# Both ends of the expert stage: first-round tables, token-order router logits, and the last pair's rows through a transposed one-hot matrix

## The chip, the cores and the metric

One core of a Trainium2 chip runs the whole program. Its engines are TensorE (PE in the profile, its weight loads PEld), VectorE (DVE), ScalarE (ACT), GpSimd (POOL) and SyncE (SP), with 16 DMA engines between SBUF and DRAM. Each engine works off its own instructions in order, and semaphores order the engines among each other. The metric is the device time of one execution in microseconds; lower is better.

## The reference, cut to what matters

Two layers over 384 tokens (128 of a prompt, 256 of a sample) of width 1024. Each layer has a mixer (layer 0: state space heads and long convolutions, layer 1: attention) and then a mixture of experts, and a final norm follows. The change is in the experts:

```python
g_prob = softmax(t @ w_gr + b_gr)                    # 4 groups
g_w, g_idx = top_k(g_prob, 1)
e_logits = (t @ w_er + b_er).reshape(n_tok, 4, 8)    # 8 experts in each group
e_prob = softmax(e_logits[g_idx])
e_w, e_idx = top_k(e_prob, 2)
weights = g_w * e_w / sum(e_w)                       # combine: (tokens, 32 experts)
hid = silu(t @ w_gate[e]) * (t @ w_up[e])            # hidden width 256
out = sum over e of (hid * combine) @ w_down[e]
x = x + gate * out                                   # gate: one row for prompt, one for sample
```

All arithmetic is fp32.

## The kernel before

Tokens lie in three tiles `t` of 128. The residual is `xR`, its normed and modulated transpose is `hT` (width on partitions).

**Head of the expert stage.** `router(l, t)` multiplies the 36 router columns `wr` (as TensorE's weights) with `hT`, so that the logits come out transposed. ACT copies them (`take_logits` on ACT) to `lgT`, and `logits(l, t)` turns them back on TensorE. DVE adds the bias (L2413) and picks for each token two experts, `ohs`, by a chain of small operations. From their sum `rmask` (`chosen`) TensorE counts each token's place within its expert, in `pos`, four fp32 matmuls against a triangle and ones. DVE makes a one-hot row of 384 slots for each token and choice (`onehots`, L2479, six operations). 72 bf16 matmuls of these with `rtok` give the table `tbl`: for each of 32 experts and six rounds of `CAP` = 64 slots the token that sits there. DVE decodes it into `tbli` (which row to gather, L2492, semaphore `table`) and `scati` (which row of the output to store to, `stores`). Meanwhile ACT writes the token rows `htok` to DRAM (`rows_out`).

**The stage.** Experts go in 16 pairs `n`, 64 slots for each of the two. Should an expert have more than 64 tokens, further rounds follow; here all pairs fit into one round (r = 8, 16 pairs). GpSimd gathers the rows of a pair to `xs` (indirect DMA). TensorE turns them (`turn`), multiplies with gate and up (`gate_up`), turns the hidden rows (`turn_hidden`) and multiplies with down (`down`). ACT and DVE share the copies from PSUM; the result of a pair is in `ob`, and GpSimd stores its rows to `outs_d` in DRAM (`scatter`, `store`; `expert_rows` in the trace). Weights come as blocks of 2 MB (three parts for each pair) on SP's queue, in `expert_loads`: `next_load` refills a place of the ring as soon as the matmuls that read it are done (`g_done`, `gu_done`, `down_done`). A third place for each part (`ahead`) and a fourth for gate (`late`) serve the first eight pairs only. In the order of SP's queue the last blocks are gate 14, up 14, down 13, gate 15, up 15, down 14, down 15.

**End of the stage.** TensorE does gate_up(15), down(14), turn_hidden(15), down(15), then spreads the residual gates (`gff`: a product of a row of ones with a gate row on one partition). GpSimd stores pairs 14 and 15. SP waits for both (`stored`) and loads all rows back by token, two for each token (`row_loads`, to `yg`). ACT weighs the first (`weigh`, L1921), DVE adds the weighed second (L2531), multiplies with the gate (L2534) and adds to `xR` (L2540), in six halves (`combine`). ACT measures the sum of squares (`measure`, `squares`), DVE makes the root (`root`), and the next layer's norm or the final norm follows. Loads of the next layer's projection wait for the last row load.

PSUM's eight banks are given out by a written plan (`bank_plan`): each job has a name, the engine that takes its result, and sometimes a bank; `open_bank` waits until the holder before is taken, `full` waits for TensorE, `took` for the taker. `link` waits for an operation of the same engine. In layer 0 the stage lies at about 585 to 850 us of the profile, in layer 1 at about 1097 to 1364 us.

## Time and profile before

| | us |
|---|---|
| median of three runs (1363.38 to 1369.64) | 1367.5 |
| profiled execution, its time | 1369.48 |
| profiled execution, its span | 1367.7 |
| PE busy | 1204.8 |
| DVE busy | 450.7 |
| ACT busy | 334.2 |
| POOL busy | 200.8 |

The time of a run is measured around the program; the span is from the first to the last instruction of the profiled execution. A busy matmul engine is not at its peak: the granted clock, 1.00 for 2.4 GHz and 0.50 for 1.2 GHz, says at what speed it ran (0.955 in the mean). An engine's busy time says little on its own; what ended an engine's wait, in the stretch in question, says what a change there is worth. A wait is shown as "idle before <- who ended it".

### The profile page before, as it was taken

Reading aid. Unit: us, or ns where it says so; the run is one execution under the profiler, and the core shown is the slowest. Engines: PE = TensorE matmul, PEld = TensorE weight load, DVE = VectorE, ACT = ScalarE, POOL = GpSimd, SP = SyncE. Lnnn points to the kernel's source line nnn. Section 1 sums busy time; section 2 is a strip of 40 time slices with the busy share of each in tenths; the row PEclk is TensorE's granted clock in tenths of the full one; section 3 lists DMA queues with packets and bytes.
Section 4 is the critical chain, followed back from the end, with each engine's and each line's share of the span. In section 5 each row is a group of like instructions: output and inputs, shape, how many; then the busy total and the mean of one; then the engine's idle time right before and its main releaser. Section 6 shows DMA issues by size and latency. Waiting matters only on the chain.

```text
span 1367.7 us, 16634 instructions
## 1 busy us (share of the span) xinstructions
PE 1204.8 (88%) x6374; PEld 677.0 (50%) x6374; DVE 450.7 (33%) x969; ACT 334.2 (24%) x850; POOL 200.8 (15%) x261
## 2 busy tenths in 40 slices
PE   4999998999999999959999775999789959989772
PEld 2456654554545554446545433753455546545430
DVE  1452078542338740431111105112573331111115
ACT  4212364210123200321111105123453321111113
POOL 1000022200125410011212102061001011212100
PEclk9999999999999999979999996999999979999996
DMA  9995510667910136369999986760315469999983
GB/s 340 347 387 192 184 31 1 229 236 252 349 62 1 62 148 247 121 233 420 417 416 419 420 367 248 284 65 0 139 63 179 172 231 420 419 416 419 419 355 146
DMA packets 94402, 336.91 MB, mean 246 GB/s; under 512 B 12784, under 2 KB 16598, under 8 KB 69633
## 3 DMA queue, kind: packets, MB, share of 16 engines
q1 hardware_dynamic: 73488, 303.18, 56.8%
q0 software_dynamic: 13952, 25.86, 6.9%
q10 hardware_dynamic: 6897, 6.97, 1.5%
q8 instruction: 45, 0.74, 0.2%
q14 instruction: 20, 0.16, 0.0%
HBM read 333.76 MB, written 23.18 MB: 261 GB/s over the span
## 4 chain that ended last, share of the span: by engine, by line
PE 70%; DMA 17%; DVE 6%; ACT 2%; POOL 2%; issue 2%; SPq 0%; ACTq 0%; DVEq 0%; POOLq 0%
PE bank L870 62%; DMA ring<-in_moe_w_down_dram 10%; PE bank L874 5%; DMA ring<-in_moe_w_up_dram 4%; PE bank L901 3%; DMA ring<-in_w_ada_dram 1%; DMA arena<-expert_rows 1%; PE bank L947 1%; POOL ring L2691 1%; POOL hT L2694 1%; DVE arena L2531 1%; DVE arena L2534 1%; ACT ring L2000 1%; DMA hT<-rows,scr 0%; POOL arena L2694 0%
## 5 line engine op out<-in xcount | busy, mean ns | idle before, releaser
L870 PE MATMUL bank<-ring,arena 128*64 128x256 f32 (+3 forms) x2624 | 439.4, 440 | 45.1 <-DMA ring<-in_moe_w_up_dram 18.2
L870 PEld LDWEIGHTS bank<-ring,arena 128*64 128x64 f32 (+1 forms) x2624 | 218.7, 146 | 229.6 <-issue 116.7
L870 PE MATMUL bank<-hT,ring 128*128 128x384 f32 (+4 forms) x960 | 301.2, 472 | 2.4 <-DVE hT L2129 1.7
L870 PEld LDWEIGHTS bank<-hT,ring 128*128 128x128 f32 (+1 forms) x960 | 177.7, 192 | 122.4 <-issue 18.0
L870 PE MATMUL bank<-arena 128*64 128x256 f32 (+7 forms) x800 | 117.3, 383 | 10.5 <-DVE arena L2479 4.5
L2506 DVE TENSOR_TENSOR hT<-hT,bank 128x256 f32<-128x256 f32 x32 | 13.5, 421 | 266.8 <-ACT hT L1887 266.8
L870 PEld LDWEIGHTS bank<-arena 128*64 128x64 f32 (+4 forms) x800 | 59.9, 150 | 52.0 <-issue 28.8
L1887 ACT ACTIVATE hT<-bank 128x256 f32<-128x256 f32 x32 | 12.3, 384 | 249.5 <-PE bank L870 249.5
L874 PEld LDWEIGHTS bank<-cst,hT 128*128 128x128 f32 x368 | 47.4, 190 | 48.0 <-issue 35.9
L874 PE MATMUL bank<-cst,hT 128*128 128x128 f32 x368 | 61.1, 301 | 11.3 <-DMA hT<-rows,scr 11.3
L870 PE MATMUL bank<-ring,hT 128*128 128x512 f32 x144 | 63.3, 599 | 0.4 <-ACT hT L2014 0.4
L2511 DVE COPY arena<-bank 128x512 f32<-128x512 f32 x32 | 22.1, 692 | 111.7 <-PE bank L870 111.7
L874 PE MATMUL bank<-cst,arena 128*128 128x128 f32 (+2 forms) x208 | 30.8, 293 | 29.3 <-DVE arena L2534 12.8
L870 PE MATMUL bank<-arena,ring 128*128 128x128 f32 (+2 forms) x272 | 46.8, 324 | 4.6 <-ACT arena L1963 1.8
L874 PEld LDWEIGHTS bank<-cst,arena 128*128 128x128 f32 (+2 forms) x208 | 25.9, 153 | 42.5 <-DVE arena L2534 14.7
L1898 ACT ACTIVATE arena<-bank 128x512 f32<-128x512 f32 x32 | 19.1, 597 | 113.6 <-PE bank L870 113.6
L870 PE MATMUL bank<-arena,cst 128*128 128x512 f32 (+5 forms) x76 | 35.3, 616 | 12.4 <-DVE arena L2452 9.4
L2749 POOL COPY scr<-arena 128x1 int32 x28 | 5.1, 182 | 271.5 <-ACT arena L1898 167.2
L870 PEld LDWEIGHTS bank<-ring,hT 128*128 128x128 f32 x144 | 27.5, 193 | 34.3 <-issue 33.3
L2733 POOL DMA_INDIRECT hT<-rows,scr x32 | 33.1, 1036 | 71.2 <-PE bank L874 27.2
L870 PEld LDWEIGHTS bank<-arena,ring 128*128 128x128 f32 (+2 forms) x272 | 32.1, 185 | 22.8 <-issue 9.2
L2739 POOL DMA_INDIRECT expert_rows<-arena,scr x32 | 32.6, 1019 | 60.1 <-POOL scr L2749 23.5
(315 smaller groups left out, 1131.9 us busy)
## 6 DMA issues: line engine op xcount, KB each, us to landing
ring<-in_moe_w_up_dram SPq DMA_DIRECT2D x28, 2048.0 KB, 20.8
ring<-in_moe_w_down_dram SPq DMA_DIRECT2D x28, 2048.0 KB, 19.5
ring<-in_w_ada_dram SPq DMA_DIRECT2D x24, 2048.0 KB, 16.0
ring<-in_moe_w_gate_dram SPq DMA_DIRECT2D x24, 2048.0 KB, 20.6
ring<-in_ev_w_in_dram SPq DMA_DIRECT2D x10, 2048.0 KB, 12.8
arena<-in_moe_w_gate_dram SPq DMA_DIRECT2D x8, 2048.0 KB, 14.6
ring<-in_ev_w_out_dram SPq DMA_DIRECT2D x4, 2048.0 KB, 17.3
arena<-in_moe_w_up_dram SPq DMA_DIRECT2D x4, 2048.0 KB, 20.3
```

What stands on the lines that cost most here:

```text
L870: return nc.tensor.matmul(out, lhsT, rhs, start=start, stop=stop_, skip_group_check=True)
L874: return nc.tensor.transpose(out, in_, ident[0:n, 0:n])
L901: last = nc.tensor.matmul(ps[32 * g:32 * g + 32, :], conds[l][:, k, at:at + 32], w[:, k, :], start=b == first and k < 4, stop=(l, b) in AD ...
L947: last = nc.tensor.matmul(ps[32 * q:32 * q + 32, :], conds[0][:, k, 22 - 2 * j:54 - 2 * j], w[:, k, :], start=j == 0 and k < 4, stop=j == ...
L1898: A_(ob[:, 0:512], banks[5][:, :], ACT.Copy).then_inc(s["d_act"], 1)
L2000: A_(prob[b][:, a, 0:w], bank("score", n, a)[:, 0:w], ACT.Exp, bias=nrows[:, b, 1, a:a + 1], scale=scale, accum_out=nrows[:, b, 2, a:a + 1 ...
L2511: COPY(ob[:, 512:1024], banks[6][:, :]).then_inc(s["d_dve"], 1)
L2531: link(STT(out=y0, in0=y1, scalar=ysw[:, NT + t:NT + t + 1], in1=y0, op0=mult, op1=add))
L2534: weighed = TT(y0, y0, bank("gff", l, v, h), mult)
L2691: nc.gpsimd.tensor_tensor(y1, y1, yadd[(3 * turn - 3 + i) % 2], ALU.add).then_inc(S("spec"), 1)
L2733: nc.gpsimd.indirect_dma_start(xs[:, b, :], None, rows_d[l], bass.IndirectOffsetOnAxis(ap=at, axis=0), bounds_check=T - 1, oob_is_err=False)\
L2739: nc.gpsimd.indirect_dma_start(outs_d[l], bass.IndirectOffsetOnAxis(ap=idxc[:, 2 + b:3 + b], axis=0), ob, None, bounds_check=2 * T - 1, oo ...
```

## The change

1. The router's operands change places: `hT` is the weights, `wr` streams, so the logits come out by token. `lgT`, ACT's copies and `logits` are gone, and `take_logits` moves ahead on DVE.
2. `rmask` and the two matrices of the position count are bf16 (`before16`, `ones16`, copied by GpSimd). `rtok` has three columns instead of two, all bf16. DVE reads `pos` directly after it has made them.
3. The one-hot rows are made for slots 0 to 63 first. Their table `tbl0` (12 matmuls, 16 entries) is decoded on its own, and the first four gathers wait for it alone. The other 320 columns, `tbl` with 60 matmuls, and the combine weights `ysw` follow.
4. Both output arrays in DRAM are filled with zeros early in layer 0's mixer (`blank`, four transfers from a zero constant).
5. The last pair's rows are not stored. DVE builds, for the last pair, one-hot rows times the combine weight (`pick_tok`), TensorE turns them, ACT copies them to `pick_slot`, and makes diagonal matrices of the first weights (`diag0`, over three constants that are no longer read). For each of six halves `last` is diag0 times the loaded first row plus pick_slot times `ob`, two fp32 matmuls into one bank. DVE adds the weighed second row and multiplies with the gate; the add to `xR` is GpSimd's for tiles 0 and 1, DVE's for tile 2.
6. TensorE's order at the end: `pick`, gates(0), down(14), gate half of gate_up(15), gates(1), up half, turn_hidden(15), down(15), `last`. The block down 14 goes to the place `ahead[2]` and is issued right after down 13; then gate 15, up 15, down 15. Row loads wait for pairs 14 and 13. Loads of the next projection don't wait for them.

The diff, cut to its core (bank names, offsets and the order of constants are left out):

```diff
+        job(("pick", l), "act", None, 7)
...
-                job(("gff", l, v, h), "dve", None, (0, 1, 6, 7)[2 * v + h])
+                job(("gff", l, v, h), "weighed", None, (0, 1, 2, 7)[2 * v + h])
+        for t in range(NT):
+            for h in range(2):
+                job(("last", l, t, h), "dve", None, (3, 4, 5, 6, 3, 4)[2 * t + h])
...
+        onehots = [area(at, NT, T // 2).bitcast(BF16) for at in (3072, 3984)]
+        rmask = area(3648, NT * E // 2).bitcast(BF16)
+        rtok = area(3696, 3 * NT * E).bitcast(BF16).rearrange("p (c t e x) -> p c t e x", c=2, t=NT, x=3)
...
-                with sp.Fori(4, r - 1) as i:
+                with sp.Fori(4, r - 2) as i:
...
-                next_load(l, 2 * r - 3, 2 * r - 1, 1, PAIRS - 1, 2)
+                m = 2 * r - 4
+                for part in range(2):
+                    next_load(l, m, m + 2, 0, PAIRS - 2, part)
+                next_load(l, m - 1, m + 1, 1, PAIRS - 3, 2)
+                sp.wait_ge(S("down_done%d" % l), len(PLACES[2]))
+                sp.dma_start(halves(expert_place(2, 2)), expert_source(l, PAIRS - 2, 2)).then_inc(expert_sem(l, 2, 2), 16)
+                for part in range(3):
+                    next_load(l, m + 1, m + 3, 1, PAIRS - 1, part)
...
-                    sp.wait_ge(S("stored%d_%d" % (l, b)), 16 * r)
+                even, odd = sp.to_reg(16 * r), sp.to_reg(16 * r - 16)
+                sp.wait_ge(S("stored%d_0" % l), even)
+                sp.wait_ge(S("stored%d_1" % l), odd)
...
+                if k + 1 == SSD_NEXT:
+                    for l in range(2):
+                        for c in range(2):
+                            sp.dma_start(outs_d[l][c * T:(c + 1) * T, :], K["k_zero"]).then_inc(S("blank"), 16)
...
-                sp.wait_ge(S("yg%d" % (NT - 1)), 16)
...
             def router(l, t):
-                ps = open_bank("rt", l, t)
+                ps = open_bank("lg", l, t)
...
-                    last = mm(ps[0:NG + E, 0:P], wr[:, k, :], hT[:, k, cols(t)], k == 0, k == KD - 1)
+                    last = mm(ps[:, 0:NG + E], hT[:, k, cols(t)], wr[:, k, :], k == 0, k == KD - 1)
...
-            def logits(l, t):
-                ps = open_bank("lg", l, t)
-                took(pe, "rt", l, t)
-                tr(ps[:, 0:NG + E], lgT[t % 2][0:NG + E, :]).then_inc(done, 1)
...
+                pe.wait_ge(S("xs0"), l + 1)
...
-                mask = rmask.rearrange("p t e -> p (t e)")
-                mm(ps[:, 0:NT * E], before, mask, True, False)
-                mm(ps[:, NT * E:(NT + 1) * E], ones, mask[:, 0:E], False, False)
...
-                        for par_ in range(2):
-                            for t in range(NT):
-                                o = ps[par_ * CAP:(par_ + 1) * CAP, 2 * PAIRS * r:2 * PAIRS * (r + 1)]
-                                rhs = rtok[:, c, t, :, :].rearrange("p (q e) x -> p e q x", e=2)[:, par_, :, :]
-                                last = mm(o, onehots[c][:, t, r * CAP:(r + 1) * CAP], rhs, c == r == t == 0, c == 1 and t == NT - 1)
-                last.then_inc(done, 1)
+                mm(ps[:, 0:NT * E], before16, rmask, True, False)
+                mm(ps[:, NT * E:(NT + 1) * E], ones16, rmask[:, 0:E], False, False)
+                mm(ps[:, E:(NT + 1) * E], ones16, rmask, False, False)
+                mm(ps[:, 2 * E:(NT + 1) * E], ones16, rmask[:, 0:2 * E], False, True).then_inc(done, 1)
+                def tables(name, rounds):
+                    ps = open_bank(name, l)
+                    for c in range(2):
+                        pe.wait_ge(S("onehot"), 4 * l + 2 * (name == "tbl") + c + 1)
+                        for r in rounds:
+                            for par_ in range(2):
+                                for t in range(NT):
+                                    at = 3 * PAIRS * (r - rounds[0])
+                                    o = ps[par_ * CAP:(par_ + 1) * CAP, at:at + 3 * PAIRS]
+                                    rhs = rtok[:, c, t, :, :].rearrange("p (q e) x -> p e q x", e=2)[:, par_, :, :]
+                                    last = mm(o, onehots[c][:, t, r * CAP:(r + 1) * CAP], rhs, c == t == 0 and r == rounds[0],
+                                              c == 1 and t == NT - 1)
+                    last.then_inc(done, 1)
...
-                n = 2 * r - 1
-                gate_up(n, 1)
-                down(n - 1, 0)
-                turn_hidden(n, 1)
-                down(n, 1)
-                for x in ("x_act", "x_dve", "ht_act", "d_act", "d_dve", "hid"):
-                    pe.wait_ge(s[x], 2 * r)
-                pe.sem_inc(done, 1)
-                pe.wait_ge(S("gff_in"), 16 * (l + 1))
-                for v in range(2):
+                def gates(v):
...
+                n = 2 * r - 1
+                pe.sem_inc(done, 1)
+                ps = open_bank("pick", l)
+                pe.wait_ge(S("picked"), l + 1)
+                for t in range(NT):
+                    last = tr(ps[:, cols(t)], pick_tok[:, t, :])
+                last.then_inc(done, 1)
+                pe.wait_ge(S("gff_in"), 16 * (l + 1))
+                pe.wait_ge(s["x_act"], n + 1)
+                pe.wait_ge(s["x_dve"], n + 1)
+                gates(0)
+                down(n - 1, 0, 2)
+                pe.wait_ge(s["hid"], n)
+                gate_up(n, 1, lambda: gates(1))
+                turn_hidden(n, 1)
+                down(n, 1)
+                pe.wait_ge(s["hid"], 2 * r)
+                pe.wait_ge(s["ht_act"], 2 * r)
+                took(pe, "pick", l)
+                for t in range(NT):
+                    for h in range(2):
+                        ps = open_bank("last", l, t, h)
+                        pe.wait_ge(S("yg0%d" % h if t == 0 else "yg%d" % t), 16 * (l + 1))
+                        if t == 1:
+                            pe.wait_ge(s[("d_act", "d_dve")[h]], 2 * r)
+                        mm(ps[:, :], diag0[:, t, :], yg[t][:, 0, wide(h)], True, False)
+                        pe.wait_ge(s[("d_act", "d_dve")[h]], 2 * r)
+                        mm(ps[:, :], pick_slot[:, t, :], ob[:, wide(h)], False, True).then_inc(done, 1)
...
+                for t in range(NT):
+                    A_(diag0[:, t, :], ident, ACT.Copy, scale=ysw[:, t:t + 1])
+                full(act, "pick", l)
+                A_(pick_slot, bank("pick", l)[:, 0:T].rearrange("p (t n) -> p t n", t=NT), ACT.Copy).then_inc(taken["act"], 1)
+                take_down(n - 1, 0, 16 * (r - 1))
...
-                take_down(n - 1, 0, 16 * (r - 1))
...
-                TT(rmask, ohs[:, 0], ohs[:, 1], add).then_inc(S("chosen"), 1)
+                TT(rmask.rearrange("p (t e) -> p t e", t=NT), ohs[:, 0], ohs[:, 1], add).then_inc(S("chosen"), 1)
...
-                    STT(out=rtok[:, c, :, :, 0], in0=over(tilestart, E), scalar=float(T * c), in1=ohs[:, c], op0=add, op1=mult)
-                    last = TS(rtok[:, c, :, :, 1], ohs[:, c], tokin[:, 0:1], None, mult)
+                    TT(rtok[:, c, :, :, 0], over(tilestart, E), ohs[:, c], mult)
+                    TS(rtok[:, c, :, :, 1], ohs[:, c], tokin[:, 0:1], None, mult)
+                    last = TS(rtok[:, c, :, :, 2], ohs[:, c], float(T * c), None, mult)
...
+                def one_hot(slots):
+                    for c in range(2):
+                        for t in range(NT):
+                            last = TS(onehots[c][:, t, slots], slotrow[:, slots], posn[:, c * NT + t:c * NT + t + 1], None, ALU.is_equal)
+                        last.then_inc(S("onehot"), 1)
+                one_hot(slice(0, CAP))
+                take(RED(cm, bank("pos", l)[:, NT * E:(NT + 1) * E], AX_X, ALU.max))
+                took(dve, "pos", l)
+                link(TS(cmp_, thr, cm, float(PAIRS // 2), ALU.is_lt, mult))
+                link(RED(cm, cmp_[:, 1:ROUNDS], AX_X, add))
+                COPY(counti[:, :], cm).then_inc(S("trips%d" % l), 1)
+                tb, sf = rsc[:, 900:996], rsc[:, 1300:1396]
+                empty = rsc[:, 1200:1296]
+                def table(name, first, n):
+                    cs = slice(first, first + n)
+                    ts = bank(name, l)[:, 0:3 * n].rearrange("p (r x) -> p r x", x=3)
+                    full(dve, name, l)
+                    link(RED(tb[:, cs], ts[:, :, 0:2], AX_X, add))
+                    link(TS(empty[:, cs], tb[:, cs], 0.0, 4096.0, ALU.is_equal, mult))
+                    STT(out=tbli[:, cs], in0=tb[:, cs], scalar=-1.0, in1=empty[:, cs], op0=add, op1=add).then_inc(S("table"), 1)
+                    link(STT(out=sf[:, cs], in0=tb[:, cs], scalar=-1.0, in1=empty[:, cs], op0=add, op1=add))
+                    take(TT(sf[:, cs], sf[:, cs], ts[:, :, 2], add))
+                table("tbl0", 0, PAIRS)
...
+                table("tbl", PAIRS, (ROUNDS - 1) * PAIRS)
...
+                link(TS(last_base, cm, float(CAP * 2 // PAIRS), None, mult))
+                TS(last_pos, posn, last_base, None, sub)
+                TT(last_w.rearrange("p (n e) -> p n e", e=2), ohs.rearrange("p c t e -> p (c t) e")[:, :, E - 2:E], over(ysw, 2), mult)
...
+                for t in range(NT):
+                    for e in range(2):
+                        for c, dst in enumerate((pick_tok, pick_slot)):
+                            i = NT * c + t
+                            last = TS(dst[:, t, e * CAP:(e + 1) * CAP], slotrow[:, 0:CAP], last_pos[:, i:i + 1], last_w[:, 2 * i + e:2 * i + e + 1],
+                                      ALU.is_equal, mult)
+                link(last)
+                TT(pick_tok, pick_tok, pick_slot, add).then_inc(S("picked"), 1)
+                take_down(n - 1, 0, 16 * (r - 1))
...
-                take_down(n - 1, 0, 16 * (r - 1))
...
+                def combine(t, h):
...
-                    for h in range(2):
-                        y0, y1 = yg[t][:, 0, wide(h)], yg[t][:, 1, wide(h)]
-                        dve.wait_ge(S("y0"), 2 * NT * l + 2 * t + h + 1)
-                        link(STT(out=y0, in0=y1, scalar=ysw[:, NT + t:NT + t + 1], in1=y0, op0=mult, op1=add))
-                        if t < 2:
-                            full(dve, "gff", l, v, h)
-                        weighed = TT(y0, y0, bank("gff", l, v, h), mult)
-                        if t != 1:
-                            take(weighed)
-                            took(dve, "gff", l, v, h)
-                        else:
-                            link(weighed)
-                        TT(xR[:, t, wide(h)], xR[:, t, wide(h)], y0, add).then_inc(S("xup"), 1)
+                    y = yg[t][:, 1, wide(h)]
+                    full(dve, "last", l, t, h)
+                    dve.wait_ge(S("yg0%d" % h if t == 0 else "yg%d" % t), 16 * (l + 1))
+                    take(STT(out=y, in0=y, scalar=ysw[:, NT + t:NT + t + 1], in1=bank("last", l, t, h), op0=mult, op1=add))
+                    took(dve, "last", l, t, h)
+                    if t < 2:
+                        full(dve, "gff", l, v, h)
+                    TT(y, y, bank("gff", l, v, h), mult).then_inc(S("weighed"), 1)
+                    dve.wait_ge(S("weighed"), 2 * NT * l + 2 * t + h + 1)
+                    if t == 2:
+                        TT(xR[:, t, wide(h)], xR[:, t, wide(h)], y, add).then_inc(S("xup2"), 1)
...
-                combine(1)
+                for t, h in ((0, 0), (0, 1), (1, 0)):
+                    combine(t, h)
...
-                combine(2)
+                combine(1, 1)
+                combine(2, 0)
...
+                combine(2, 1)
...
-                    pool.wait_ge(S("table"), l + 1)
...
-                for b in range(2):
-                    n = 2 * r - 2 + b
...
+                store(0)
+                for t in range(2):
+                    for h in range(2):
+                        pool.wait_ge(S("weighed"), 2 * NT * l + 2 * t + h + 1)
+                        nc.gpsimd.tensor_tensor(xR[:, t, wide(h)], xR[:, t, wide(h)], yg[t][:, 1, wide(h)], ALU.add)\
+                            .then_inc(S("xup"), 1)
```

## Rows read from the trace of the kernel before

**Rows 1.** The page's first line.
```profile
span 1367.7 us, 16634 instructions
```
**Rows 2.** Busy us by stretch: PE, PEld, DVE, ACT, POOL, clock, DMA share, GB/s.
```profile
595.00:600.00 5.00, 2.11 (x72) 2.04 (x72) 2.70 (x12) 0.00 (x0) 0.54 (x1) 0.50 0.01 3
...
650.00:700.00 50.00, 50.00 (x370) 27.85 (x368) 7.22 (x12) 7.41 (x16) 9.74 (x16) 1.00 1.02 418
```
**Rows 3.** Timeline of DVE, layer 0, head: start us, us, instruction, idle before.
```profile
585.18 0.20 DVE L2413 TENSOR_TENSOR arena<-bank,scr 128x36 f32<-128x36 f32 x1 [3.25 <-PE bank L874]
...
590.47 0.26 DVE L2452 TENSOR_TENSOR arena<-arena 128x96 f32<-128x96 f32 x1
...
593.86 2.06 DVE L2479 TENSOR_SCALAR arena<-scr,arena 128x384 bf16<-128x384 f32 x6
...
598.28 0.26 DVE L2492 TENSOR_TENSOR scr<-arena 128x96 int32<-128x96 f32 x1
```
**Rows 4.** Timeline of PE, layer 0 (the first row from the mixer).
```profile
144.34 1.03 PE L870 MATMUL bank<-scr,rstd 128*128 128x16 f32 x8 [0.81 <-ACT rstd L1664]
...
581.97 1.91 PE L870 MATMUL bank<-hT,arena 128*36 128x128 f32 x16 [0.35 <-DVE arena L2413]
...
590.87 1.94 PE L870 MATMUL bank<-arena,cst 128*128 128x96 f32 x8 [4.71 <-DVE arena L2452]
595.08 2.11 PE L870 MATMUL bank<-arena 128*64 128x32 bf16 x72 [2.27 <-DVE arena L2479]
602.90 1.97 PE L874 MATMUL bank<-cst,hT 128*128 128x128 f32 x8 [5.70 <-DMA hT<-rows,scr]
```
**Rows 5.** Timeline of SP's queue: start us, us, issue.
```profile
143.59 98.36 SPq L739 DMA_DIRECT2D ring<-in_w_ada_dram x2
...
611.14 0.37 SPq L786 DMA_DIRECT2D ring<-in_moe_w_gate_dram x1
```
**Rows 6.** Timeline of PE, end of the stage (last row: layer 1).
```profile
801.02 3.65 PE L870 MATMUL bank<-ring,arena 128*64 128x512 f32 x16 [0.81 <-DMA ring<-in_moe_w_down_dram]
804.61 0.51 PE L874 MATMUL bank<-cst,hT 128*128 128x128 f32 x2
...
821.83 3.65 PE L870 MATMUL bank<-ring,arena 128*64 128x512 f32 x16 [0.82 <-DMA ring<-in_moe_w_down_dram]
826.83 6.31 PE L870 MATMUL bank<-arena,cst 1*128 1x512 f32 x8 [1.34 <-DVE arena L2511]
...
850.39 4.31 PE L870 MATMUL bank<-hT,ring 128*128 128x128 f32 x32
...
1334.07 3.65 PE L870 MATMUL bank<-ring,arena 128*64 128x512 f32 x16 [0.82 <-DMA ring<-in_moe_w_down_dram]
```
**Rows 7.** Timeline of DVE, layer 0, end of the stage.
```profile
804.82 0.69 DVE L2511 COPY arena<-bank 128x512 f32<-128x512 f32 x1 [3.87 <-PE bank L870]
...
834.34 0.75 DVE L2531 SCALAR_TENSOR_TENSOR arena<-arena,scr 128x512 f32<-128x512 f32 x1 [8.02 <-ACT arena L1921]
...
846.99 0.69 DVE L2540 TENSOR_TENSOR xR<-xR,arena 128x512 f32<-128x512 f32 x1
```
**Rows 8.** Timeline of POOL and of SP's queue, layer 0, end of the stage.
```profile
827.18 0.97 POOL L2739 DMA_INDIRECT expert_rows<-arena,scr x1 [3.74 <-DVE arena L2511]
...
829.91 0.89 SPq L829 DMA_DIRECT2D arena<-expert_rows x2
```
**Rows 9.** Busy time by microsecond, columns as in rows 2.
```profile
609.00:610.00 1.00, 1.00 (x10) 0.69 (x8) 0.00 (x0) 0.00 (x0) 0.00 (x0) 0.88 0.96 406
...
827.00:828.00 1.00, 1.00 (x3) 0.46 (x3) 0.00 (x0) 0.72 (x2) 0.82 (x1) 0.85 0.00 0
...
1343.00:1344.00 1.00, 1.00 (x3) 0.48 (x2) 0.00 (x0) 0.00 (x0) 0.00 (x0) 0.55 0.77 199
```
**Rows 10.** One line's instructions (ns min/median/max), and the page's group of 512-column products.
```profile
L2694 POOL TENSOR_TENSOR hT<-hT,ring x6: 1267/1276/1659, 414.9 to 463.9; 128x512 f32<-128x512 f32 x6
...
L870 PE MATMUL bank<-ring,hT 128*128 128x512 f32 x144 | 63.3, 599 | 0.4 <-ACT hT L2014 0.4
```

146 lines of the change are left out of this document (57 added, 89 removed).

## The prediction

> **What bounds the kernel now.** I first read the page. The profiled execution spans 1367.7 us [rows 1], and the chain of work that ended last is mostly TensorE, with the expert weights' transfers as the second part. That mean hides three stages with different limits, so I went to busy time by stretch. In the middle of the expert stage the 16 DMA engines are full (share 1.02, 418 GB/s) [rows 2]: 48 weight blocks of 2 MB per layer set that stretch. Just ahead of it, at 595 to 600 us, the DMA share is 0.01 [rows 2]: the blocks for which there is room have landed, and every other place is freed only by a matmul of the first pair. The stream resumes at 611.14, when the gate matmuls of pair 0 are done [rows 5]. So each microsecond taken from the routing ahead of the first gather moves the whole saturated stream, and what hangs behind it. After the last weight block (821.83) no transfer of weights is left either: down matmuls, store, row loads and the combine follow in series [rows 6 to 8]. Head and end of the stage are latency, the middle is bandwidth. The change touches head and end, in both layers.
>
> **Part 1, head.** In layer 0 the third tile's logits are added at 585.18 [rows 3]. The router that made them ended at 581.97+1.91 = 583.88 [rows 4]; between them lay an ACT copy and a TensorE transpose. In token order both go. The router itself now loads 128x128 weights and streams 36 columns. The nearest row, 8 instructions with 128x128 weights and 16 columns, takes 1.03 us [rows 4], so 16 take 2.0 against 1.91: no change. The add starts at about 584.0: 1.2 us gained.
>
> The chain on DVE to the chosen mask (590.47+0.26) is unchanged, so the mask stands at 589.5. Two more small table inputs (six operations instead of four, pitch about 0.17 us) end at 590.5. The position matmuls took 1.94 us for 8 fp32 instructions [rows 4] and sat exposed: DVE went on only after them. Now they are 4 in bf16. The price has no row; it lies between the bf16 table matmuls (2.11/72 = 0.03 each) and the fp32 ones (0.24 each), so 0.1 to 1.0 us; I take 0.6, nearer to the bf16 row in kind and to the other in width. They then hide behind the six table inputs, and another 1.2 us goes (2.4).
>
> The one-hot rows: six operations of 384 columns take 2.06 us [rows 3]. For the first round they are 64 columns wide. Bounds: 0.12 us (the small operations' pitch) and 0.34 us each; I take 0.13, so 0.8 in all, and 1.25 us more goes (3.65). The other 320 columns are made after the first table. Of the 72 table matmuls (2.11 us) [rows 4] 12 stand ahead of the first table; before, DVE had to wait for the rest. They now lie under the count of the rounds, another 0.65 (4.3). Decoding: five operations, 1.3 us up to 598.28+0.26 [rows 3], become three on 16 columns, 0.7 us shorter. The first table stands at about 593.5 instead of 598.54: **5.0 us**. With fp32 prices for the position matmuls it is 4.0, with everything at its low bound 5.5.
>
> What comes next: GpSimd's gather waits for the table and for the token rows in DRAM, whose transfers end before the DMA share is 0.01 [rows 2], that is before 595. The time from table to first transpose, 602.90-598.54 = 4.36 us [rows 3, 4], stays. The remaining tables take DVE until about 598.6 (six operations of 320 columns 1.75, five weight operations 1.0, decoding and last-pair tables 2.1); its first row copy is wanted at 597.9+1.97 = 599.9, so they are hidden by 1.3 us. The late weight block waits for the second gather (599.4) and for this decoding, and moves 5 us too. The same rows stand about 511.6 us later in layer 1. Head: 2 x 5.0 = **10.0 us**.
>
> **Part 2, stores and loads.** The 6.3 MB of zeros go out behind a block issued at 143.59 whose successor is held until about 241 [rows 5]; the DMA engines are nearly idle for most of that time, and the first store comes 480 us later. Cost nothing; uncovered it would be about 15 us (6.3 MB at 418 GB/s). The down block of pair 14 goes to another place and no longer waits for a down matmul. The DMA engines are full at that time anyway, and the last block still waits for pair 13's down matmuls (801.02+3.65), so I keep its landing at 821.83 [rows 6]. The first block of the next projection no longer waits for the rows; TensorE reaches it late, nothing gained.
>
> **Part 3, end of the stage.** I follow layer 0 without the head's shift. DVE frees its down copy at 804.82+0.69 = 805.5 [rows 7], then makes 12 one-hot operations of 64 columns (0.12 to 0.34 each; I take 0.14, so 1.7) and one add of 384 columns (0.6): 807.9. TensorE has ended turning at 805.1 [rows 6] and now stands before `picked`: a new wait of 2.8 us, with gates, down(14) and gate_up(15) queued behind it. Then: three transposes 0.4; gates(0) 1.8 (two products; an fp32 instruction of 512 columns takes 63.3/144 = 0.44, two per product [rows 10]); down(14) 3.65; gate half 3.67; gates(1) 1.8; up half 3.67. That is 822.9, after the landing of the last block. Silu, product, turn and copy are no longer covered by down(14): 2.2 us with hops. down(15) runs 825.1 to 828.8, against 825.5 now: **3.3 us later**.
>
> From there the path is shorter. Before: store issue at 827.18, row loads at 829.91, first combine at 834.34, last add over at 846.99+0.69 = 847.7 [rows 7, 8]. After: only pair 14 is stored. Its copies end at 814.6, the store starts at 815.5, and even at 8 us landing (the median of such stores under full load; this last one took 2.7) and 3.7 for the row load, the first rows are there by 827.2. Each half tile then needs two products, 1.8 us: the first is ready at 830.6, the last at 839.6. DVE needs 1.45 us per half (two operations) and GpSimd 1.27 for the add (median 1.276) [rows 10]. The critical order is (1,1): product 836.0, DVE 838.7, GpSimd 840.1, ACT's squares and root 841.3, scaling 842.0, then the third tile's last half, 2.1: **844.1**, 3.6 us earlier. The next layer's first tile follows 1.4 later, at 845.5 against 850.39 [rows 6]: 4.9 gained. In layer 1 the landing is 512.24 later (1334.07), the combine ends there at 1360.5, and the same sum gives 4.2.
>
> GpSimd's adds take 1.27 us where DVE's take 0.69 [rows 7, 10], so the move lengthens each add by 0.6; it leaves DVE free for the next half. The Trainium skill, GPSIMD Engine Reference, section 8 (Key points), says that GpSimd shares its SBUF interfaces with VectorE and contends with operations that have two SBUF inputs, and that VectorE is about twice as fast elementwise. The second agrees with the row. By the first, adds beside DVE could be slower than 1.27; the longest GpSimd add in that row is 1.66, which would put 0.4 on the (1,1) step alone.
>
> **The clock in that wait.** The granted clock fell from 2.4 to 1.2 GHz 2.4 us after the last expert matmul in layer 0 (825.48 to 827.9), within the one-row gate products, and in layer 1 after 5.4 us (1337.7 to 1343.1), again within them [rows 6, 9]; three more falls stand after 2.7 to 3.5 us without matmuls. The new wait, transposes and gates(0) are 5.0 us of the same kind. Once low, it rose 6.3 us after the transposes of 602.90 [rows 4, 9]. A fall there would double gates(0) (+1.8) and cost half of up to 6.3 us after it: 3.2 to 4.9, I take 4.2. The tail's gain is then 0.7 and 0. The Trainium skill, TensorE: Matmul & The Clock Gate, section "HAM oscillation — how this bites in real kernels", says that a wait between short bursts of matmuls throttles the array and that the next burst pays again. By that rule both tails pay, 8.4 us in all. These rows make a fall likely (I say 0.6 per layer), not certain.
>
> **Sum.** Head 10.0. Tails, with 0.6 for a fall in each layer: 9.1 with no fall (0.16), 4.9 with one (0.48), 0.7 with both (0.36), which alone would give 1356.8. I take the middle of one and both, 3: in all 13. The profiled run took 1369.5 (1367.7 and 1.8 around it), so 1356.5; it lies 2.0 over the median of 1367.5, so **1354.5**.
>
> **Rivals.** (a) The clock holds in both layers: 19.1 gained, 1348.4. For it: the clock held through waits of 1.9 us all along the stream. Against it: every longer stretch shown ends in a fall. (b) The head's gain stops at something else: the token rows land only at 597 rather than before 595, or the position matmuls cost as fp32 and the one-hots 0.34 each. Then a head gives about 2 us, in all 7: 1360.5. Against it: the DMA share at 595. (c) The end of the stage is a loss: 0.34 us for each of the 12 one-hot operations (+2.4), a fall of the clock at its dearest (+4.9) and slower adds (+0.4) on top, so each tail is 3 us later than now: gain 10-6 = 4, 1363.5. (d) The other sign: the clock stays at 1.2 GHz from the `picked` wait to the end of the combine, and does not come back in the gaps around up(15). The full-speed work there is 28.9 us (1.8+3.65+3.67+1.8+3.67+3.65 and 10.7 for the combine), which doubles: +28.9-4.5 per layer, 1367.5-10+49 = 1406. It decides from 18 us of half speed per layer on. Against it: the rise after 6.3 us. (e) The change does not do what it says, that is the stream's middle absorbs the head and the end is as long: no change. The share of 1.02 speaks against it.
>
> **Chances.** Forecast 0.52 (its own range 1351 to 1358), (a) 0.15, (b) 0.13, (c) 0.12, (d) 0.03, (e) 0.05. Range: 1346.5, below (a) by its bounds, to 1361.5, above (b). Half a per cent, 6.8 us, is about what a measurement of this kernel can tell from no change. Faster by more: forecast, (a) and nearly all of (b), 0.81. Same: (c), (e), 0.15. Slower: (d) and what I don't see, 0.04.
>
> **What would show it.** Right: the first gather 5 us earlier in both layers with the first weight reload moved as much; position matmuls under 1 us; TensorE idle 2.8 us at `picked`; down(15) ending later after the last landing; no store after it; six product pairs of 1.8 us. Wrong: a gather that waits for rows although the table stands; a clock at 0.5 through the combine; row loads landing after 829; a DMA share under 1 in the stream's middle; the last block landing later than 821.8 less the head's gain.

## The result and the profile after

The changed kernel takes 1361.8 us (median of 20 runs, 1353.7 to 1367.3) against 1368.5 (20 runs beside it): ratio 0.9949, 95% interval 0.9933 to 0.9964. That is 4.9 to 9.2 us, 6.7 at the median, half of the 13 forecast and just outside the range (1361.5). The profiled execution spans 1359.9 us, 7.8 less than [rows 1].

Not all of those 7.8 us are the change's. The windows ahead of the zero fills, where no engine's work is changed, already differ; the columns are the stretch, its length, busy time of PE, PEld, DVE, ACT and POOL, granted clock, DMA share and GB/s. Before:

```profile
40.00:80.00 40.00, 38.49 (x145) 21.07 (x138) 21.16 (x40) 12.00 (x36) 1.78 (x2) 0.96 0.98 352
80.00:120.00 40.00, 40.00 (x189) 23.51 (x188) 17.15 (x33) 9.23 (x27) 0.00 (x0) 0.93 0.92 336
```

After:

```profile
40.00:80.00 40.00, 38.49 (x154) 21.22 (x143) 22.22 (x41) 12.01 (x36) 1.78 (x2) 1.00 1.02 362
80.00:120.00 40.00, 40.00 (x192) 23.03 (x191) 16.94 (x35) 10.53 (x28) 0.00 (x0) 0.96 0.92 337
```

The clock was granted at 0.96 and 0.93 in one run and 1.00 and 0.96 in the other, so the layer's last stretch ahead of the routing is reached about 2.1 us earlier by luck (a transpose group of TensorE starts at 558.63 instead of 560.70). To read the change alone I line both traces up at VectorE's reciprocal of the third tile, just ahead of the routing (before 578.29 and 1089.93, after 575.85 and 1085.90: 2.44 and 4.03 us apart). This hides a little of the change itself, since the routers of the first two tiles stand ahead of that reciprocal. From the second tile's reciprocal to the third's it is 10.26 us in layer 0 and 16.67 in layer 1 before, and 9.99 and 16.40 after, so 0.27 us per layer belongs to the head and not to luck:

```profile
575.85 0.16 DVE L2107 RECIPROCAL small<-small 128x1 f32<-128x1 f32 x1 [1.18 <-ACT small L1679]
1085.90 0.16 DVE L2107 RECIPROCAL small<-small 128x1 f32<-128x1 f32 x1 [1.18 <-ACT small L1679]
```

The head of layer 0 on TensorE, then two rows of layer 1 (start, time, engine, line, operation; in brackets the idle time before it and what ended it):

```profile
573.04 1.87 PE L888 MATMUL bank<-arena,hT 128*128 128x36 f32 x16
576.91 1.06 PE L892 MATMUL bank<-cst,arena 128*128 128x128 f32 x8 [1.99 <-ACT arena L1684]
...
579.53 3.60 PE L888 MATMUL bank<-arena,hT 128*128 128x36 f32 x16
...
588.86 0.40 PE L888 MATMUL bank<-arena,scr 128*128 128x96 bf16 x4 [2.28 <-DVE arena L2481]
591.13 0.76 PE L888 MATMUL bank<-arena 128*64 128x48 bf16 x12 [1.87 <-DVE arena L2500]
594.06 1.99 PE L888 MATMUL bank<-arena 128*64 128x48 bf16 x60 [2.17 <-DVE arena L2500]
597.89 1.94 PE L892 MATMUL bank<-cst,hT 128*128 128x128 f32 x8 [1.84 <-DVE arena L2520]
600.67 9.47 PE L888 MATMUL bank<-ring,arena 128*64 128x256 f32 x64 [0.83 <-ACT arena L1914]
...
1090.45 1.95 PE L888 MATMUL bank<-arena,hT 128*128 128x36 f32 x16
...
1107.30 1.94 PE L892 MATMUL bank<-cst,hT 128*128 128x128 f32 x8 [2.11 <-DMA hT<-rows,scr]
```

The same router takes 1.87 us for tile 2, 3.60 for tile 3 and 1.95 in layer 1. The windows say why; in layer 0 the clock halves at 578.15 while it still has to run:

```profile
577.00:578.00 1.00, 1.00 (x10) 1.00 (x11) 0.00 (x0) 0.37 (x2) 0.00 (x0) 1.00 1.00 426
578.00:579.00 1.00, 1.00 (x8) 0.99 (x6) 0.99 (x4) 1.00 (x4) 0.00 (x0) 0.57 0.98 418
...
605.00:606.00 1.00, 1.00 (x10) 0.71 (x8) 0.00 (x0) 0.00 (x0) 0.00 (x0) 0.77 0.89 344
```

Before, it fell at 588.76. In layer 1 it fell earlier, at 1086.75, and was back at 1090.1, just as that router started. VectorE's logits, first table and last step of the second table (L2520), GpSimd's first gather, and the first weight reload on the SP queue:

```profile
583.16 0.20 DVE L2442 TENSOR_TENSOR arena<-bank,scr 128x36 f32<-128x36 f32 x1 [3.78 <-PE bank L888]
592.56 0.17 DVE L2518 SCALAR_TENSOR_TENSOR scr<-arena 128x16 int32<-128x16 f32 x1
597.20 0.24 DVE L2520 TENSOR_TENSOR arena<-arena,bank 128x80 f32<-128x80 f32 x1
```

```profile
593.65 1.22 POOL L2787 DMA_INDIRECT hT<-rows,scr  x1 [5.20 <-DVE scr L2518]
```

```profile
606.72 0.37 SPq L793 DMA_DIRECT2D ring<-in_moe_w_gate_dram  x1
```

Against [rows 3 to 5], and with the shifts of 2.44 and 4.03 taken off, the gain along the head is (us):

| reached | forecast | layer 0 | layer 1 |
|---|---|---|---|
| third tile's logits | 1.2 | -0.4 | 0.4 |
| first table | 5.0 | 3.4 | 4.2 |
| first transposes | 5.0 | 2.6 | 3.1 |
| first weight reload | 5.0 | 2.0 | 3.2 |
| down products of pair 13 | 5.0 | 2.0 | 3.6 |

With the 0.27 that the alignment hides, each entry of the two right columns is 0.3 higher. From logits to table both layers gain 3.8, the forecast's sum; what is lost lies on either side of it. The stream carries the rest whole, as forecast.

The end of the stage, layer 0, on TensorE; the last two rows are down(14) and down(15) of layer 1:

```profile
796.55 3.65 PE L888 MATMUL bank<-ring,arena 128*64 128x512 f32 x16 [0.82 <-DMA ring<-in_moe_w_down_dram]
800.13 0.50 PE L892 MATMUL bank<-cst,hT 128*128 128x128 f32 x2
804.46 0.87 PE L892 MATMUL bank<-cst,arena 128*128 128x128 f32 x3 [3.82 <-DVE arena L2573]
805.26 3.77 PE L888 MATMUL bank<-arena,cst 1*128 1x512 f32 x4
808.96 5.97 PE L888 MATMUL bank<-arena 128*64 128x512 f32 x16
814.77 3.62 PE L888 MATMUL bank<-ring,arena 128*64 128x256 f32 x32
818.32 1.98 PE L888 MATMUL bank<-arena,cst 1*128 1x512 f32 x4
820.23 3.67 PE L888 MATMUL bank<-ring,arena 128*64 128x256 f32 x32
825.01 0.50 PE L892 MATMUL bank<-cst,hT 128*128 128x128 f32 x2 [1.11 <-DVE hT L2549]
826.03 3.65 PE L888 MATMUL bank<-ring,arena 128*64 128x512 f32 x16 [0.52 <-issue]
...
846.78 1.39 PE L888 MATMUL bank<-hT,ring 128*128 128x128 f32 x6
...
1318.49 5.50 PE L888 MATMUL bank<-arena 128*64 128x512 f32 x16
...
1335.09 3.65 PE L888 MATMUL bank<-ring,arena 128*64 128x512 f32 x16 [0.52 <-issue]
```

And VectorE, which makes what TensorE waits for, then the last add:

```profile
800.95 2.77 DVE L2570 TENSOR_SCALAR arena<-scr,arena 128x64 f32<-128x64 f32 x12
803.75 0.56 DVE L2573 TENSOR_TENSOR arena<-arena 128x384 f32<-128x384 f32 x1
...
844.23 0.69 DVE L2590 TENSOR_TENSOR xR<-xR,arena 128x512 f32<-128x512 f32 x1
```

The clock falls in that wait and is back late in down(14):

```profile
802.00:803.00 1.00, 0.00 (x0) 0.00 (x0) 1.00 (x6) 0.07 (x1) 0.62 (x1) 1.00 1.02 401
803.00:804.00 1.00, 0.00 (x0) 0.00 (x0) 0.96 (x5) 0.00 (x0) 0.56 (x2) 0.71 0.96 401
...
813.00:814.00 1.00, 1.00 (x6) 0.33 (x4) 0.00 (x0) 0.00 (x0) 0.00 (x0) 0.67 0.51 213
```

From the start of pair 13's down products to the end of down(15) was 825.48-801.02 = 24.5 us [rows 6] and is 829.68-796.55 = 33.1: 8.7 longer. From there to the next layer's first tile it was 24.9 and is 17.1: 7.8 shorter. The end of layer 0 loses 0.9 us. Layer 1 goes the same way, 46.9 to 47.1 from pair 13's down products to the last add, and loses 0.2. In the profiled pair the accounts close: 2.2 luck, 2.3 and 3.9 heads (with the 0.27 each), -0.9 and -0.2 ends, 0.5 elsewhere, 7.8 in all.

### The profile page after: what moved, and what is told of

Read it like the earlier page. It is cut to its first block, busy times and chain, and to the rows that moved or that the text cites. A ratio compares the mean times of both kernels' runs of the same rounds, so it can differ in the third digit from the quotient of the medians.

```text
span 1359.9 us, 16756 instructions
## 1 busy us (share of the span) xinstructions
PE 1225.6 (90%) x6414; PEld 686.9 (51%) x6414; DVE 457.1 (34%) x1019; ACT 328.7 (24%) x840; POOL 209.4 (15%) x269
## 4 chain that ended last, share of the span: by engine, by line
PE 72%; DMA 14%; DVE 6%; POOL 3%; ACT 2%; issue 2%; SPq 0%; POOLq 0%; ACTq 0%; DVEq 0%
PE bank L888 64%; DMA ring<-in_moe_w_down_dram 8%; PE bank L892 5%; DMA ring<-in_moe_w_up_dram 3%; PE bank L919 3%; DMA ring<-in_w_ada_dram 1%; PE bank L965 1%; POOL ring L2743 1%; POOL hT L2746 1%; ACT ring L2029 1%; POOL arena L2746 0%; DMA arena<-in_hy_freq_dram 0%; DVE arena L2570 0%; DVE arena L2610 0%; POOL arena L2703 0%
## 5 line engine op out<-in xcount | busy, mean ns | idle before, releaser
L888 PE MATMUL bank<-ring,arena 128*64 128x256 f32 (+3 forms) x2592 | 429.9, 436 | 37.9 <-DMA ring<-in_moe_w_up_dram 14.3
L888 PEld LDWEIGHTS bank<-ring,arena 128*64 128x64 f32 (+1 forms) x2592 | 215.9, 146 | 218.4 <-issue 114.8
L888 PE MATMUL bank<-arena 128*64 128x256 f32 (+8 forms) x856 | 142.0, 410 | 14.4 <-DVE arena L2500 8.1
L888 PEld LDWEIGHTS bank<-arena 128*64 128x64 f32 (+4 forms) x856 | 68.1, 153 | 71.9 <-issue 47.2
L892 PEld LDWEIGHTS bank<-cst,hT 128*128 128x128 f32 x368 | 50.5, 198 | 41.6 <-issue 38.4
L892 PE MATMUL bank<-cst,arena 128*128 128x128 f32 (+3 forms) x214 | 31.8, 294 | 28.0 <-DMA cst<-in_k_cst_dram 9.4
L892 PEld LDWEIGHTS bank<-cst,arena 128*128 128x128 f32 (+3 forms) x214 | 26.9, 153 | 40.1 <-issue 18.8
L888 PEld LDWEIGHTS bank<-ring,hT 128*128 128x128 f32 x144 | 27.5, 193 | 34.1 <-issue 33.1
L888 PE MATMUL bank<-arena,cst 128*128 128x512 f32 (+2 forms) x84 | 42.8, 629 | 0.3 <-ACT arena L1817 0.3
L2703 POOL TENSOR_TENSOR arena<-arena,scr 128x512 f32<-128x512 f32 x12 | 14.7, 1228 | 170.7 <-DVE arena L2225 147.8
```

The costliest lines, as they stand in the source:

```text
L888: return nc.tensor.matmul(out, lhsT, rhs, start=start, stop=stop_, skip_group_check=True)
L892: return nc.tensor.transpose(out, in_, ident[0:n, 0:n])
L2703: nc.gpsimd.tensor_tensor(m2, cbb[:, q // 2, :].unsqueeze(1).to_broadcast([P, 4, P]), dts[:, 1, t, hs].unsqueeze(2).to_broadcast([P, 4, P] ...
```

## The experiments

Each was timed in five rounds; ratios are to the kernel before, which ran beside it. "Against the change" is the difference from 1361.8, whose own uncertainty is about 2 us.

**1. Each half alone.** Two kernels divide the diff. `head_only` takes the edits of the router, the masks, the one-hots and the tables; `tail_only` the zero fills, the loads of pair 14, the last pair's matrix and the combine.

```
head_only:  + job(("tbl0", l), "dve") ... table("tbl0", 0, PAIRS); one_hot(slice(CAP, T))
            (stores of both last pairs, weigh() and combine(t) as before)
tail_only:  + job(("pick", l), "act", None, 7) ... down(n - 1, 0, 2); combine(t, h)
            (router, pos and one table "tbl" as before; last_pos and last_w made behind it)
```

> Only the head of the stage is changed (router, short position masks, first table alone); rows of the last pair are stored and combined as before. Theory: the traces of before and after, lined up at the last reciprocal ahead of the router's last tile, show a head that gives 2.0 us in layer 0 and 3.1 to 3.6 in layer 1, because the clock falls while the router still runs (578.4 instead of 588.1), and because the first transposes also wait for the second table. So about 5.5 us less than before: ratio 0.996, some 1363. The last layer-0 weight reload of the head is about 2 us earlier against that reciprocal. Rival: the head is worth the 10 us of the forecast and the end of the stage takes half of it away: ratio 0.9925, some 1358.

> Only the end of the stage is changed (zero fills, last pair combined by the one-hot product); the head is that of before. Theory: the end gives nothing; in the changed kernel's trace, from the last stream-paced down product of pair 13 to the end of the combine, it is 0.9 us longer in layer 0 and 0.2 us longer in layer 1. So within 0.2% of before, 1367 to 1371, with the clock at 1.2 GHz from the wait for the one-hot matrix through gates(0) and most of down(14). Rival: the end gives the 3 us of the forecast (1365.5) or, if a quieter head lets it start in another clock phase, the 9 us of the case without a fall (1359).

Measured: head_only 1361.2, ratio 0.9946 (0.9928 to 0.9965); tail_only 1367.6, ratio 0.9992 (0.9976 to 1.0007). The head alone is worth what the whole change is, 7 us (4.8 to 9.9), with 10 just outside; the end gives nothing that can be told from zero (-1.0 to 3.3). So the rival in which a good head is eaten by a bad end is out. The 3 us forecast for the tails are not ruled out by these times, as they lie just inside the interval; it is the traces, with -0.9 and -0.2 us, that speak against them.

**2. Keep TensorE busy in the wait for the one-hot matrix.**

```diff
                 ps = open_bank("pick", l)
+                for _ in range(28):
+                    tr(ps[:, 0:P], ident)
                 pe.wait_ge(S("picked"), l + 1)
```

> The changed kernel with 28 repeated 128x128 transposes of the identity (results overwritten, about 3.4 us) in TensorE's wait for the one-hot matrix. Theory: the clock's fall in that wait is what costs, not the wait itself. With the engine busy the granted clock stays 1.00 there, gates(0) takes 2.0 instead of 3.77 us and down(14) 3.65 instead of 5.97 (5.50 in layer 1), so 4.1 and 3.7 less per layer: 1354 against the changed kernel's 1361.8, ratio to before 0.989. Rival: the fall comes anyway (the transposes do not hold it, or it falls within the gates, which are one-row products), and nothing changes: 1361.8, ratio 0.995.

Measured: 1356.3, ratio 0.9918 (0.9898 to 0.9937): 5.5 less than the change, where 7.8 was expected. TensorE in layer 0, then layer 1:

```profile
799.58 3.22 PE L892 MATMUL bank<-cst 128*128 128x128 f32 x28
803.47 0.55 PE L892 MATMUL bank<-cst,arena 128*128 128x128 f32 x3 [0.68 <-DVE arena L2575]
803.95 2.03 PE L888 MATMUL bank<-arena,cst 1*128 1x512 f32 x4
805.90 5.26 PE L888 MATMUL bank<-arena 128*64 128x512 f32 x16
...
1310.07 1.98 PE L888 MATMUL bank<-arena,cst 1*128 1x512 f32 x4
1311.98 3.65 PE L888 MATMUL bank<-arena 128*64 128x512 f32 x16
```

In layer 1 the whole cost of the fall is gone (5.50 to 3.65 and 3.78 to 1.98). In layer 0 the gates run at full speed, but the clock falls behind them (granted 0.88 in 805 to 806, 0.50 in the next microsecond) and down(14) pays. So the fall is shown to be the price, and the one-row products (1x512) did not prevent it in layer 0, although the profile counts the engine as busy in them; in layer 1 the clock held through them. By the Trainium skill, TensorE: Matmul & The Clock Gate, section "HAM oscillation — how this bites in real kernels", waits between short bursts are what throttles; the runs agree, with all eight such waits (four kernels with the order of the change, two layers each) ending in gates of 3.77 or 3.78 us.

**3. Let down(14) cover the wait.**

```diff
+                down(n - 1, 0, 2)
                 ps = open_bank("pick", l)
                 pe.wait_ge(S("picked"), l + 1)
...
                 gates(0)
-                down(n - 1, 0, 2)
                 pe.wait_ge(s["hid"], n)
-                gate_up(n, 1, lambda: gates(1))
+                gate_up(n, 1)
+                gates(1)
```

> The changed kernel with TensorE's order at the end of the stage changed: down(14) first, then the three transposes of the one-hot matrix and gates(0), both halves of gate_up(15), gates(1), turn, down(15). Theory: what the end loses is this order. down(14) covers the making of the one-hot matrix (3.65 against 3.8 us of waiting), the clock stays at 1.00, and TensorE needs 3.65+0.8+2.0+3.67+3.67+2.0+0.6 = 16.4 us from the start of down(14) to that of down(15): 801.0 to 817.4, which is when the last weight block lands (816.7), instead of 826.0. So 8.6 us less per layer, 1361.8-17 = 1345, ratio 0.983. Rival: TensorE is not what holds the end: pair 14's store and the row loads behind it (or ScalarE, whose copies of down(14) wait behind the one-hot copy) come late and the combine starts when the rows land; then under 4 us per layer, 1354 or more.

Measured: 1350.2, ratio 0.9864 (0.9843 to 0.9886): 11.6 less than the change, two thirds of the 17 expected. From the start of pair 13's down products to the end of down(15) it is 28.8 and 25.7 us in the two layers instead of 33.1 and 32.7. Layer 0 on TensorE:

```profile
801.80 3.65 PE L888 MATMUL bank<-arena 128*64 128x512 f32 x16 [1.16 <-DMA arena<-in_moe_w_down_dram]
...
813.46 3.67 PE L888 MATMUL bank<-ring,arena 128*64 128x256 f32 x32 [2.02 <-DMA ring<-in_moe_w_up_dram]
817.07 1.98 PE L888 MATMUL bank<-arena,cst 1*128 1x512 f32 x4
...
820.00 5.35 PE L888 MATMUL bank<-ring,arena 128*64 128x512 f32 x16 [0.52 <-issue]
```

The wait for the matrix is gone. What I had missed: the up weights of pair 15 land only at 813.4, so TensorE waits 2.0 us for them, and the clock falls behind the gates once more, 1.7 us on down(15). Rows came late only in layer 1, by 0.46.

**4. Fill that second wait with the gates.** As 3, but with the gates where the change has them.

```diff
-                gate_up(n, 1)
-                gates(1)
+                gate_up(n, 1, lambda: gates(1))
```

> As down_first (down(14) ahead of the one-hot transposes), but gates(1) back between the two halves of gate_up(15), where TensorE waited 2.0 us in layer 0 for the up weights. Theory: in down_first the wait there and the one-row gates behind the up half together let the clock fall at 820.6, so that down(15) took 5.35 instead of 3.65. Now gates(1) fills the wait, turning the hidden rows starts 0.8 us earlier in layer 0, the clock holds and down(15) takes 3.65: 2.5 us less than down_first in layer 0, nothing in layer 1 (its wait was 0.56): 1347.7, ratio 0.984. Rival: the one-row products let the clock fall wherever they stand (in tail_busy it fell in them at 805.9): then up(15) or down(15) pays it and the time is that of down_first, 1350.

Measured: 1350.4, ratio 0.9874 (0.9846 to 0.9901). The place behaves as expected, down(15) takes 3.65 in layer 0, and from pair 13's down products to its end it is 26.2 us instead of 28.8. The median does not show it: in layer 1 the same path is 0.5 longer, and in this profile the clock was low from 580.2 to 607.5, nearly all of layer 0's head. Whether it is worth anything over 3 stays open.

**5. Keep TensorE busy ahead of the third tile's transposes.**

```diff
                     ps = open_bank("xn", which, t, h)
+                    if which in ("ffn0", "ffn1") and (t, h) == (2, 0):
+                        for _ in range(14):
+                            tr(ps[:, 0:P], ident)
```

> The changed kernel with 14 repeated transposes of the identity (results overwritten, about 1.7 us) in the wait of 1.99 us ahead of the third tile's transposes, in both layers. Theory: that wait, 1.65 us before the change (the logits' transposes stood in it), is what lets the clock fall at 577 to 578.5 while the router still has to run; with the engine busy it stays at 1.00 until about 588, the router takes 1.9 instead of 3.6 us (2.0 to 2.2 in other runs of the same head), its neighbours 1.1 per tile, and the first table comes 0.9 to 1.7 us earlier per layer: 2 to 3 us in all, 1359 to 1360, ratio 0.9935. Rival: the fall does not hang on that wait (or filling it delays the transposes as much as the clock gives): 1361.8, ratio 0.995, with the fall at the same place.

Measured: 1362.3, ratio 0.9961 (0.9945 to 0.9977): nothing gained. The mechanism was borne out and its worth was wrong. Layer 0, TensorE and GpSimd:

```profile
576.99 1.87 PE L888 MATMUL bank<-arena,hT 128*128 128x36 f32 x16
...
583.41 1.95 PE L888 MATMUL bank<-arena,hT 128*128 128x36 f32 x16 [0.68 <-DVE hT L2121]
...
601.34 1.95 PE L892 MATMUL bank<-cst,hT 128*128 128x128 f32 x8 [3.25 <-DMA hT<-rows,scr]
```

```profile
596.90 1.08 POOL L2790 DMA_INDIRECT hT<-rows,scr  x1 [6.35 <-DMA rows<-arena]
```

The clock held until 585.4, in layer 1 past 1097, and the router took 1.95 in both. Counted from the second tile's router (576.99 here, 573.04 in the change) the first table is 1.7 us earlier: it starts its last step at 594.78, 17.8 behind, against 19.5. But the gather starts 19.9 behind against 20.6, since now it waits for the token rows in DRAM, and the reload follows at 33.4 against 33.7. In layer 1 the gather waits for the rows too. So with the clock held there, the table gains 1.7 us, the gather only 0.7 and the reload 0.3, because the next limit, the rows, stands close behind: they share full DMA engines with two weight blocks.

**6. Turn the first pair without waiting for the second table.**

```diff
                 for b in range(8):
-                    took(pe, *held[b])
+                    if b != 4:
+                        took(pe, *held[b])
...
                 turn(0, 0)
+                took(pe, "tbl", l)
```

> The changed kernel, but TensorE waits for VectorE's copy of the second table only after the first pair's transposes (they use other banks). Theory: the 0.8 to 1.0 us between the landing of the first gather (packets end at 596.9 and 1105.9) and the first transposes (597.89, 1107.30) is this wait. Without it they start 0.5 us earlier in layer 0 and about 1 in layer 1, and the stream with them: 1.5 us in all, 1360.3, ratio 0.994. Rival: the gather itself lands 0.8 to 1.0 later after its table than before (4.3 instead of 3.4), by transfers or GpSimd; then the start stays and the wait is put down to the transfer.

Measured: 1361.7, ratio 0.9954 (0.9938 to 0.9971), no difference. In layer 0 the first transposes start 4.7 us after the first table stands (592.08 to 596.76), against 5.2 in the change (592.73 to 597.89): the wait was real and 0.5 long. In layer 1 nothing moves (gather to transposes 4.43 and 4.42), which bears the rival out there: the gather lands late by itself. Why it does is not settled. Its GpSimd instruction took 1.08 or 1.09 in both layers of before and 1.20 to 1.32 in 12 of the 16 heads of the new kind (two for each of eight kernels). VectorE's 320-column one-hots beside it don't settle it, as they ran beside a gather of 1.08 in layer 1 of the change too; from its start to the first transposes it is 3.4 to 5.8 us in the traces, which varies more than that.

**7. Everything busy.** 4 and 6 together, the filler of 5, and more transposes of the identity ahead of the positions, the two tables and the first pair.

```diff
                 ps = open_bank("pos", l)
+                for _ in range(26):
+                    tr(ps[:, 0:P], ident)
...
                     ps = open_bank(name, l)
+                    for _ in range(12 if name == "tbl0" else 14):
+                        tr(ps[:, 0:P], ident)
...
+                for _ in range(10):
+                    tr(banks[0][:, 0:P], ident)
                 turn(0, 0)
```

> gates_between and early_turn together, with TensorE kept busy in every wait of the head by transposes of the identity (14 ahead of the third tile, 26 ahead of the positions, 12 and 14 ahead of the two tables, 10 ahead of the first pair). Theory: the head's waits are what hold its clock at 1.2 GHz from 588 to 605; with them filled the first pair's transposes take 1.1 instead of 1.94 and gate_up(0) 7.2 instead of 9.1 to 9.5, so 2.9 us more per layer than what the third tile's filler gives. In all 1347.7-1.5-2.5-5.8 = 1338, ratio 0.978. Rival: fillers that run past the end of their wait delay the tables, or the weights of pair 0 and 1 then hold the stream: 1343 or more.

Measured: 1344.2, ratio 0.9835 (0.9804 to 0.9866): 6.2 less than 4, where 9.8 was expected, and the best version here. Layer 0:

```profile
595.10 1.05 PE L892 MATMUL bank<-cst,hT 128*128 128x128 f32 x8
597.51 7.13 PE L888 MATMUL bank<-ring,arena 128*64 128x256 f32 x64 [1.35 <-DVE arena L2555]
```

Transposes of 1.05 instead of 1.94 and gate_up(0) of 7.13 instead of 9.47: that is 3.2 of the 3.7 us by which the first reload comes earlier after the second tile's router (29.95 instead of 33.68). Part of the expected gain fell to the rows, for which the gather waits in both layers, and in layer 0 to a filler: the clock fell at 589.8, the 14 transposes ahead of the second table ran until 592.7, and VectorE's one-hots for it had been ready at 591.3. How the rest divides is not shown.

## Why the prediction was wrong

**The head, 10.0 forecast, 6.2 in the profile, 7.0 timed alone.** Most terms hold. The position matmuls take 0.40 us (0.6 assumed, 0.1 to 1.0 bounded). The short one-hots take 1.06 for six, 0.18 each, inside 0.12 to 0.34 and nearer the low end. From logits to table the sum is right, 3.8. Two steps failed. "The add starts at about 584.0: 1.2 us gained" priced the router from rows at full clock, which is right (1.87 and 1.95), but left out that removing the logits' transposes lengthens the wait ahead of the third tile from 1.65 to 1.99 us, and that the clock then falls by the time of that tile's transposes: 2.3 and 0.9 us after the reciprocal in the two layers, instead of 10.5 and 10.8. The logits gain -0.15 and 0.6, counted with what stands ahead of the reciprocal, instead of 1.2. In the new head the clock fell so early in 11 of 12 cases (six kernels, two layers), in none of the four with the old head (before and tail_only), and in none of the four with the wait filled. That the 0.34 us alone do it is not shown. "The time from table to first transpose [...] stays" did not hold: 5.2 and 5.3 instead of 4.4 and 4.3, about 0.5 of the 0.8 excess in layer 0 being the second table, which I had moved behind the gather on VectorE without naming TensorE's wait for all eight banks. Layer 0 pays another 0.6 in gate_up(0), at half clock for longer. Rival (b), the head stopped by the token rows, is the nearest in kind, though in the change itself they were there in time; they become the limit once the clock holds.

**The end, 3 forecast, -1.1 in the profile, 0.6 (-1.0 to 3.3) timed alone.** The mechanism was named: the new wait, the gates at half clock and down(14) behind them. (The prediction puts the fall in layer 0 of before at 827.9; it stands at 827.7, which changes nothing.) Priced at 4.2, a fall cost 4.1 and 3.7 (experiment 2's terms: 1.8 on gates(0), 2.3 and 1.9 on down(14)). The combine is right to a tenth: 15.3 us from down(15) to the last add forecast, 15.2 measured; down(15) ending 8.7 later is 3.3 and 4.2 as forecast and 1.2 of a size that was off. That size is the price of the 12 small one-hot operations, 0.23 us each for "I take 0.14", inside its bounds, so the wait was 3.8 instead of 2.8. The step that failed is "I take the middle of one and both, 3": a fall had 0.6 per layer, and it came in eight of eight. (The mean by the stated chances would have been 4.1, further off.) The case with both falls, 0.7 and 0, less 1.0 each for the one-hots, is what happened in the sum, -1.3 against -1.1. By layer it is -0.3 and -1.0 against -0.9 and -0.2, so that the sum fits so well is partly luck.

**The rest.** The zero fills cost nothing: tail_only, which has them, reaches the head within 0.1 us of before. The stream carried the head's gain. The row loads are in time: the last store starts at 816.63, and VectorE's combine waits for TensorE's product, not for rows. GpSimd's adds took 1.26 to 1.27 us beside VectorE. This does not test the contention that the Trainium skill, GPSIMD Engine Reference, section 8 (Key points), speaks of: it names VectorE operations with two SBUF inputs (or in a 2-port perf mode, which no trace here shows), and of those that ran beside the adds none took two tiles from SBUF: the scalar_tensor_tensor and the multiply took one of theirs from a PSUM bank. By the sum of 10 and 3 I expected 1354.5, counted from 1367.5. Before ran at 1368.5 beside the change, so 1.0 of the miss is that base, and 6.2 to 7.0 off it and nothing for the ends give 1361.5 to 1362.3.

## What to carry to other kernels

Price the clock with the wait: where an edit opens or lengthens an idle stretch of TensorE, read what the engine did before each fall already in the trace, and work out what follows at half speed as a case of its own, with a chance taken from how often such waits ended in a fall. Before placing a new wait, ask which ready work could stand in front of it: here the same instructions in another order gave 11.6 us where the change had given 6.7. And when a chain is shortened, look up the second-latest input of its consumer (here all banks, and rows in DRAM): it caps the gain.

## What the runs showed of the hardware

Dummy transposes help to hold the clock: with the waits filled (and the end reordered), the mean granted clock of the profiled execution rose from 0.964 to 0.984. They don't make it certain: in layer 0 of all_busy it still fell at 579.6 and at 589.8. One-row products are no safe cover: they count as busy for 2 us, and the clock fell within or behind them in before, tail_busy (layer 0), down_first (layer 0) and, in layer 1, all_busy (at 1303.2, with no wait of TensorE since 1296.4; the gate half behind gates(0) took 5.36). It held through them in both layers of gates_between. The scatter of the times often goes with the clock: over the 20 executions of the changed kernel the span goes with the mean granted clock, from 1363.2 us at 0.959 to 1351.2 at 0.971 (correlation -0.91); over 12 of tail_only it is -0.90, over six of down_first and six of gates_between it does not show (0.19, -0.07). Two single profiles can differ by several us for reasons that lie outside the change.
